# A decoder layer on one core: the two up-projections computed as three rounded products per block, delta net's first, with the samples' attention fold between two of their units

## The chip, the core and the metric

The kernel runs on one core of a Trainium2 chip. The core has five engines with instruction streams of their own: TensorE (PE, matrix products into the accumulator PSUM), VectorE (DVE), ScalarE (ACT), GpSimd (POOL) and SyncE (SP, which here only issues DMAs). They wait for each other by semaphores. The metric is the device time of one execution in microseconds (us): 2939.98 us, the median of 3 runs (2938.37 to 2940.77).

## What is computed

One layer of a hybrid decoder for 256 prompt tokens and 8 sample tokens, which go through all dense products together as T = 264 columns. Cut to what matters here:

```python
proj = rmsnorm(x) @ w_in                      # q, k, v, gates of both branches
o_fox = fox attention of the prompt, and of the samples against a paged cache
o_gdn = gated delta net, rmsnorm per head, times silu(z)
ga = sigmoid(proj[..., OFF_GATE:OFF_GATE + D_MODEL])
gb = sigmoid(proj[..., OFF_GATE + D_MODEL:N_IN])
m = ga * (o_fox @ w_up_fox) + gb * (o_gdn @ w_up_gdn)   # the two up-projections
x = x + m @ w_out
x = x + peer_ffn(rmsnorm(x))                  # routing, 16384 experts: "u" and "v"
x = x + sigmoid(rmsnorm(x) @ w_ple_gate) * (p @ w_ple)
```

`w_up_fox` and `w_up_gdn` are 1024 x 2048 each, `w_out` is 2048 x 2048.

## The kernel before

All activations lie transposed: 128 features on the partitions, the 264 tokens along a row. A dense product is worked off in units of 1 MB of weights (128 partitions x 2048 values). SP loads the units one after the other into a ring of four slots `WR`, in the order of the table `STREAM`: "A" (56 units), "gates" (32), "up" (16), "out" (16), "wq" (16), "u" (128), "v" (128), "ple" (16).

Nearly all of the stream is **split**. A unit is cut into four quarters of 512 columns. ACT writes each quarter rounded to fp32r into the buffer `ckh` (`high_part`, L431), DVE writes the rest, weight minus rounded weight, into `ckl` (`low_part`, L436), and PE makes three products for each block of 128 x 128: high by high, high by low, low by high (`products`, L626 to L628), on an input that is split in the same manner (`hh3`, `hl3`, in the tile `split`). There is one set of `ckh` and `ckl`: `high_part` of a quarter waits until PE has done with this quarter of the unit before (`quarter_done`), `low_part` waits for `hi_ready`, and PE waits for `lo_ready`. So a unit's high and low parts are made while PE works on the unit before it, a quarter behind.

The 16 units of "up" alone are not split. PE multiplies the unsplit float32 weights of the ring slot by the unsplit branch outputs `ot3` (L1050): of each unit 8 blocks are fox's and 8 delta net's, into two PSUM banks. Each unit makes one tile of 128 output features. DVE then multiplies both banks by their gates (L1895, L1896), adds them (L1899), ACT rounds the sum (L1307) and DVE makes its low part (L1901): the split input of "out". Only after the last tile does PE start "out" (`mt_ready`).

Just before "up", the attention of the samples is finished. PE multiplies the last pair of value pages (`value_pair(31)`, L946), DVE picks the rows (`value_rows(7)`, L1848 and L1851), PE folds them (job `sot`, L1038, 8 products with 8 columns each, which the trace shows as 16), DVE adds the sample's own value (L1879) and gives `of_ready`, for which PE, POOL (which then loads x again, L1429) and DVE wait.

What runs is fixed by the order in which each engine's program is written; a table of jobs gives the PSUM bank of each (`bank(n)` is bank n mod 4), and a job waits until the bank's last user, four jobs before, has been read (`claim`, `evac`). `rounded` is a second fp32r tile; while the gates run, its memory (under the name `early`) holds the recurrent states of the samples.

Of the kernel before, what the change touches and what calls it, by code (L numbers as in the profile page):

```python
# [49 lines left out]
for _name, _c in STREAM:  # L50
# [6 lines left out]
        22: [("gns", 1)], 23: [("gn0", 4)], 24: [("gn1", 4)], 31: [("sot", 1)]}  # L57
# [11 lines left out]
JOB_LIST += [("up", 16), ("out", 16),  # L69
            ("norm1", 1), ("wq", 16), ("key", 9), ("u", 128), ("norm2", 1), ("ple", 16)]  # L70
JOB = {}
SPLIT_JOBS = ("A", "out", "wq", "u", "ple") + tuple(f"gate{_u}" for _u in range(32))
# [10 lines left out]
def split_index(s):  # L83

    return s if s < S0["up"] else s - 16
# [69 lines left out]
def build(nc, xT, pT, wd, vd, wsmall, wple, subk, kx, vx, lx, state, convst, params, consts, ptab,  # L155
          o_x, o_k, o_v, o_lf, o_sp, o_ss, o_cs):
    with ExitStack() as ctx:
# [46 lines left out]
        as_f32 = lambda ap: ap.bitcast(F32)  # L204
        hh3 = sp_(HH, KT * T).rearrange("p (k t) -> p k t", t=T)
# [125 lines left out]
        merged, mh_ready = sem("merged"), sem("mh_ready")  # L331
        ws_hi, ws_lo = sem("ws_hi"), sem("ws_lo")
# [84 lines left out]
        def wait_slot(eng, it, m, s, back=0):  # L417

            if S0["up"] <= s < S0["out"]:
                eng.wait_ge(pe_job, it * m + (PJ[JOB["up"] + s - S0["up"]] - back))  # L420
            else:
                eng.wait_ge(lo_ready, it * (4 * m) + 4 * (split_index(s) + 1 - back))
# [186 lines left out]
        def _(pe):  # L609
# [20 lines left out]
            def split_unit(it, m, s, n, mj=4, h0=None):  # L630
# [4 lines left out]
                for q in range(RING):  # L635
                    wait_low_part(pe, it, m, s, q)
                    for kk in range(QK):
                        k = q * QK + kk
                        if h0 is not None:
                            pe.wait_ge(ht_ready, h0 + k + 1)  # L640
                        last = products(bank(n)[:, 0:T], ckh(q)[:, kk * P:(kk + 1) * P], ckl(q)[:, kk * P:(kk + 1) * P],
                                        hh3[:, k, :], hl3[:, k, :], k == 0, k == KT - 1)
                    last.then_inc(quarter_done, 1)

            def dense(name, its, h0=None):
                with pe.Fori(0, its) as it:
                    for j in range(RING):
                        split_unit(it, 4, S0[name] + j, JOB[name] + j, h0=None if j else h0)
# [385 lines left out]
            n = JOB["sot"]  # L1034
            claim(pe, n)
            pe.wait_ge(on_ready, NS)
            for s in range(NS):
                last = mm(bank(n)[:, s * NH:(s + 1) * NH], at(ON + s * P, P), cst(C_FOLD, NH), start=True, stop=True)  # L1038
            last.then_inc(pe_job, 1)


            pe.wait_ge(of_ready, 1)
            with pe.Fori(0, 4) as it:
                for j in range(RING):
                    n = JOB["up"] + j
                    pe.wait_ge(w_loaded[j], it * 16 + 16 * (S0["up"] // 4 + 1))
                    pe.wait_ge(evac[n % 4], it + n // 4)
                    for half in range(2):
                        for k in range(NH):
                            last = mm(ps[:, n % 4 + 4 * half, 0:T], wr(j)[:, (half * NH + k) * P:(half * NH + k + 1) * P],  # L1050
                                      ot3[:, half * NH + k, :], start=(k == 0), stop=(k == NH - 1))
                    last.then_inc(pe_job, 1)
            pe.wait_ge(mt_ready, 1)
            dense("out", 4)
# [63 lines left out]
        def _(act):  # L1118
# [161 lines left out]
            for u in range(32):  # L1280
# [13 lines left out]
                if u == 21:  # L1294
                    act.wait_ge(og_ready, 1)
                    wait_done(act, JOB["sgo13"] + 1)
                    for h in range(NH):
                        A(at(GSQ + h * T, T), blk(OT, NH + h), ACT.Square).then_inc(bsq_ready, 1)
                if u == 22:
# [4 lines left out]
            with act.Fori(0, 4) as it:  # L1304
                for j in range(RING):
                    act.wait_ge(merged, it * 4 + (j + 1))
                    A(split[:, bass.ds(it * (4 * T) + (HH + j * T), T)], at(TMU + (j % 2) * 2 * T, T), ACT.Copy).then_inc(mh_ready, 1)  # L1307
# [158 lines left out]
        def _(dve):  # L1466
# [387 lines left out]
            for u in range(32):  # L1854
# [20 lines left out]
            wait_evac(dve, JOB["spb"])  # L1875
            ch(V.tensor_tensor(at(OTMP, 64), at(VS, 64), at(PSF, 64), ALU.mult))
            n = JOB["sot"]
            wait_done(dve, n)
            V.tensor_tensor(ot3[:, 0:8, SEQ:T], hs(OTMP), bank(n)[:, 0:64].rearrange("p (s h) -> p h s", h=NH),  # L1879
                            ALU.add).then_inc(of_ready, 1)  # L1880
            dve.wait_ge(of_ready, 1)
            dve.sem_inc(evac[n % 4], 1)
            wait_evac(dve, JOB["gate31"])


            dve.wait_ge(of_ready, 1)
            V.memset(at(ZT, T), 0.0).then_inc(zero_tile, 1)
            with dve.Fori(0, 4) as it:
                for j in range(RING):
                    n = JOB["up"] + j  # L1890
                    dve.wait_ge(pe_job, it * 4 + PJ[n])
                    ga = arena[:, bass.ds(it * (4 * T) + (GT + j * T), T)]
                    gb = arena[:, bass.ds(it * (4 * T) + (GT + (16 + j) * T), T)]
                    m, t = at(TMU + (j % 2) * 2 * T, T), at(TMU + ((j % 2) * 2 + 1) * T, T)
                    V.tensor_tensor(t, gb, ps[:, 4 + n % 4, 0:T], ALU.mult).then_inc(mg_step, 1)  # L1895
                    V.tensor_tensor(m, ga, ps[:, n % 4, 0:T], ALU.mult).then_inc(evac[n % 4], 1)  # L1896
                    dve.wait_ge(mg_step, it * 8 + (2 * j + 1))
# [281 lines left out]
```

## Time and profile before

| | us |
|---|---|
| median of 3 runs | 2939.98 (2938.37 to 2940.77) |
| the profiled execution, its own time | 2936.59 |
| span of its trace, first to last instruction | 2934.9 |
| PE busy in the span | 2809.5 (96%) |
| DVE busy | 1784.8 (61%) |
| ACT busy | 1229.0 (42%) |
| POOL busy | 593.5 (20%) |

All times below are us from the start of the span. Busy shares are means over stages that differ, so the stages are read one by one: the gates end at about 926, "up" runs from 937 to 1054, "out" from 1058 to about 1152. In the rows, L with a number is the line of the kernel before; `ps` is PSUM, `arena` the large float32 tile, and an idle time in square brackets stands with the instruction that ended it and its releaser. The float32 product of L1050 is shown as two records for each block (512 for 256 blocks); a split block is three records, one for each of L626, L627 and L628. The granted clock of PE is 1.00 at 2.4 GHz and 0.50 at 1.2 GHz.

### The profile page before, as it was taken

The numbers are of one execution on the slowest core, as the hardware profiler recorded it, in microseconds if no ns is written. First come the engines' busy times: TensorE is split into PE (matmuls) and PEld (weight loads), VectorE is DVE, ScalarE is ACT, GpSimd is POOL, SyncE is SP. The second block draws the span as 40 slices with busy tenths as digits, with TensorE's granted clock in tenths as the row PEclk, the third lists the DMA queues.
The fourth block names the chain that finished last, engine by engine and source line by source line (L and its number), as shares of the span: only waits on it lengthen the run. The fifth ranks groups of instructions, "written<-read, shape, count | busy, mean of one in ns | idle before, by whom it ended". The sixth has DMA issues, their size and how long they took to land.

```text
span 2934.9 us, 57573 instructions
## 1 busy us (share of the span) xinstructions
PE 2809.5 (96%) x22051; PEld 2681.2 (91%) x22051; DVE 1784.8 (61%) x3445; ACT 1229.0 (42%) x2123; POOL 593.5 (20%) x457
## 2 busy tenths in 40 slices
PE   6999989989999998999999999996999999999989
PEld 5999957878877887999999999996999999999989
DVE  4467545655353245458886444443788888888854
ACT  4455432023332024444545444443444444444454
POOL 2100012000000000000477677773011111111000
PEclk8999969989999999999999999998999999999999
DMA  5455415545765466755677777776565666666533
GB/s 195 177 185 182 175 64 187 200 163 205 285 251 225 144 215 203 260 187 205 199 211 208 199 206 206 198 208 219 202 231 216 229 223 223 229 233 229 206 119 121
DMA packets 167186, 588.78 MB, mean 201 GB/s; under 512 B 53474, under 2 KB 86514, under 8 KB 114098
## 3 DMA queue, kind: packets, MB, share of 16 engines
q1 hardware_dynamic: 103234, 539.96, 52.1%
q0 software_dynamic: 45808, 26.10, 5.0%
q10 hardware_dynamic: 18048, 21.50, 2.1%
q8 instruction: 52, 0.85, 0.1%
q14 instruction: 44, 0.36, 0.0%
HBM read 543.36 MB, written 44.13 MB: 200 GB/s over the span
## 4 chain that ended last, share of the span: by engine, by line
PE 74%; POOL 14%; DMA 5%; issue 4%; DVE 3%; ACT 0%; SPq 0%; DVEq 0%; POOLq 0%; ACTq 0%
PE ps L626 20%; PE ps L627 19%; PE ps L628 19%; POOL gates L1439 14%; PE ps L1050 4%; DMA gates<-arena 4%; PE ps L860 2%; PE ps L946 1%; PE ps L702 1%; PE ps L686 1%; PE ps L621 1%; PE ps L847 1%; DVE arena L1479 1%; PE ps L983 1%; PE ps L678 1%
## 5 line engine op out<-in xcount | busy, mean ns | idle before, releaser
L436 DVE TENSOR_TENSOR split<-arena,split 128x512 fp32r<-128x512 f32 x1568 | 1140.2, 730 | 790.4 <-ACT split L431 780.0
L431 ACT ACTIVATE split<-arena 128x512 fp32r<-128x512 f32 x1568 | 987.3, 631 | 1259.7 <-PE ps L628 1259.3
L626 PE MATMUL ps<-split 128*128 128x264 f32 x4224 | 1216.9, 288 | 47.1 <-DVE split L436 41.6
L627 PE MATMUL ps<-split 128*128 128x264 f32 x4224 | 1207.0, 286 | 0.0
L628 PE MATMUL ps<-split 128*128 128x264 f32 x4224 | 1205.9, 285 | 0.0
L626 PEld LDWEIGHTS ps<-split 128*128 128x128 f32 x4224 | 806.0, 191 | 72.8 <-DVE split L436 35.6
L627 PEld LDWEIGHTS ps<-split 128*128 128x128 f32 x4224 | 806.7, 191 | 0.5
L628 PEld LDWEIGHTS ps<-split 128*128 128x128 f32 x4224 | 802.4, 190 | 0.0
L626 PE MATMUL ps<-rounded,split 128*128 128x264 f32 x2048 | 583.4, 285 | 26.5 <-DVE rounded L2057 26.5
L627 PE MATMUL ps<-rounded,split 128*128 128x264 f32 x2048 | 583.7, 285 | 0.0
L628 PE MATMUL ps<-rounded,split 128*128 128x264 f32 x2048 | 580.0, 283 | 0.0
L1439 POOL DMA_INDIRECT gates<-arena x264 | 436.1, 1652 | 421.4 <-DVE arena L2032 246.1
L626 PEld LDWEIGHTS ps<-rounded,split 128*128 128x128 f32 x2048 | 386.3, 189 | 26.7 <-issue 26.7
L627 PEld LDWEIGHTS ps<-rounded,split 128*128 128x128 f32 x2048 | 386.2, 189 | 0.0
L628 PEld LDWEIGHTS ps<-rounded,split 128*128 128x128 f32 x2048 | 385.7, 188 | 0.0
L2069 DVE TENSOR_TENSOR arena<-arena,ps 128x264 f32<-128x264 f32 x512 | 216.8, 423 | 0.0
L1462 POOL TENSOR_TENSOR arena<-arena 128x1056 f32<-128x1056 f32 x32 | 78.8, 2464 | 646.7 <-DMA arena<-gates 646.7
L1050 PE MATMUL ps<-arena 128*128 128x264 f32 x512 | 117.0, 391 | 0.7 <-DVE arena L1879 0.7
L1050 PEld LDWEIGHTS ps<-arena 128*128 128x128 f32 x512 | 98.4, 193 | 18.9 <-issue 0.8
L462 POOL DMA_DIRECT2D arena<-in_vx x32 | 16.9, 528 | 273.6 <-PE ps L946 240.3
L1387 POOL MEMSET early<- 128x3088 f32 x1 | 2.7, 2671 | 274.9 <-PE ps L628 274.9
L1307 ACT ACTIVATE split<-arena 128x264 f32 x16 | 6.8, 423 | 122.8 <-DVE arena L1899 122.8
(314 smaller groups left out, 1591.0 us busy)
## 6 DMA issues: line engine op xcount, KB each, us to landing
arena<-in_wd SPq DMA_DIRECT2D x280, 1024.0 KB, 5.6
arena<-in_vd SPq DMA_DIRECT2D x128, 1024.0 KB, 4.8
arena<-in_kx SPq DMA_DIRECT2D x64, 512.0 KB, 4.6
gates<-arena ACTq DMA_DIRECT2D x32, 528.0 KB, 3.2
acts<-arena SPq DMA_DIRECT2D x32, 528.0 KB
arena<-acts SPq DMA_DIRECT2D x32, 528.0 KB, 5.8
arena<-gates SPq DMA_DIRECT2D x32, 528.0 KB, 6.8
arena<-in_vx SPq DMA_DIRECT2D x32, 512.0 KB, 6.7
```

Source lines behind the costliest of these rows:

```text
L431: nc.scalar.activation(ckh(q), at(WR + (s % 4) * D_MODEL + q * QW, QW), ACT.Copy).then_inc(hi_ready, 1)
L436: nc.vector.tensor_tensor(ckl(q), at(WR + (s % 4) * D_MODEL + q * QW, QW), as_f32(ckh(q)), ALU.subtract).then_inc(lo_ready, 1)
L621: last = mm(bank(n)[:, 0:T], ones, blk(SQ, k), start=(k == 0), stop=(k == KT - 1))
L626: mm(out, wh, xh, start=start, stop=False)
L627: mm(out, wh, xl, start=False, stop=False)
L628: return mm(out, wl, xh, start=False, stop=stop)
L678: last = mm(bank(n)[0:count, 0:T], cst(C_SEL + 15 - b, count), at(base + (b % 4) * T, T), start=(b == 0), stop=(b == count - 1))
L860: last = mm(bank(n)[:, i * P:(i + 1) * P], at(lhs + o, P), at(rhs + o, P), start=True, stop=True)
L1050: last = mm(ps[:, n % 4 + 4 * half, 0:T], wr(j)[:, (half * NH + k) * P:(half * NH + k + 1) * P], ot3[:, half * NH + k, :], start=(k == 0), ...
L1439: pool.indirect_dma_start(gate_rows, bass.IndirectOffsetOnAxis(at(places, 1).bitcast(U32), 0), at(values, 1), None, compute_op=ALU.add).th ...
L1462: nc.gpsimd.tensor_tensor(a, a, at(WBUF + b * GRP, GRP), ALU.mult).then_inc(prod_ready, 1)
L2069: V.tensor_tensor(xt3[:, d, :], xt3[:, d, :], ps[:, 4 + q, 0:T], ALU.add).then_inc(y_added, 1)
```

## The change

"up" becomes part of the split stream, and `split_index` counts its units like all others. The host lays its weights out anew: 8 units of delta net's weights, then 8 of fox's. A unit now has 16 blocks of one branch, 8 for each of two tiles of output features, so it makes two jobs (`upg0` to `upg7`, `upf0` to `upf7`, two each).

The inputs have to be split for this. Delta net's: ACT copies 128 x 2112 values into `rounded` after gate 27 (the states that lay there must have been saved by then), DVE subtracts after gate 29's low parts. Fox's: ACT copies 128 x 2112 into `split`, DVE subtracts there (`attention_out`). This input is complete only when the samples' attention is; the fold `sot` now stands on PE behind unit 1 of delta net's half (`own_rows`).

In delta net's half DVE multiplies each tile by its gate in place. In fox's half it multiplies, adds delta net's part, and ACT and DVE split the sum as before. The split sum lies in two tiles now (`merged_high`, `merged_low`: blocks 0 to 7 in `split`, 8 to 15 in `rounded`).

```diff
-            pe.wait_ge(of_ready, 1)
-            with pe.Fori(0, 4) as it:
-                for j in range(RING):
-                    n = JOB["up"] + j
...
-                            last = mm(ps[:, n % 4 + 4 * half, 0:T], wr(j)[:, (half * NH + k) * P:(half * NH + k + 1) * P],
-                                      ot3[:, half * NH + k, :], start=(k == 0), stop=(k == NH - 1))
...
+            def up_unit(name, s, xh, xl):
+                for q in range(RING):
+                    n = JOB[name] + q // 2
+                    if q % 2 == 0:
+                        claim(pe, n)
+                    wait_low_part(pe, 0, 0, s, q)
+                    for kk in range(QK):
+                        k = (q % 2) * QK + kk
+                        last = products(bank(n)[:, 0:T], ckh(q)[:, kk * P:(kk + 1) * P], ckl(q)[:, kk * P:(kk + 1) * P],
+                                        xh(k), xl(k), k == 0, k == NH - 1)
+                    last.then_inc(quarter_done, 1)
+
+            pe.wait_ge(ol_split, 1)
+            for u in range(8):
+                up_unit(f"upg{u}", S0["up"] + u, lambda k: rd_(AH + k * T, T), lambda k: rd_(AL + k * T, T))
+                if u == 1:
+                    own_rows()
+            pe.wait_ge(ol_split, 2)
+            for u in range(8):
+                up_unit(f"upf{u}", S0["up"] + 8 + u, lambda k: hh3[:, k, :], lambda k: hl3[:, k, :])
...
+            for q in range(RING):
+                high_part(act, 0, 0, S0["up"], q)
+            for u in range(16):
+                for q in range(RING if u < 15 else 0):
+                    high_part(act, 0, 0, S0["up"] + u + 1, q)
+                if u == 2:
+                    act.wait_ge(of_ready, 1)
+                    A(sp_(HH, NH * T), at(OT, NH * T), ACT.Copy).then_inc(oh_split, 1)
+                for b in range(2 * (u - 8), 2 * (u - 8) + 2) if u >= 8 else ():
+                    act.wait_ge(merged, b + 1)
+                    A(merged_high(b), at(TMU + b % 2 * 2 * T, T), ACT.Copy).then_inc(mh_ready, 1)
...
+            def attention_out():
...
+                V.tensor_tensor(ot3[:, 0:8, SEQ:T], hs(OTMP), bank(n)[:, 0:64].rearrange("p (s h) -> p h s", h=NH),
+                                ALU.add).then_inc(of_ready, 1)
...
+                dve.wait_ge(oh_split, 2)
+                V.tensor_tensor(sp_(HL, NH * T), at(OT, NH * T), as_f32(sp_(HH, NH * T)), ALU.subtract).then_inc(ol_split, 1)
+                V.memset(at(ZT, T), 0.0).then_inc(zero_tile, 1)
+
+            for u in range(8):
+                for q in range(RING):
+                    low_part(dve, 0, 0, S0["up"] + u + 1, q)
+                for i in range(2):
+                    n, b = JOB[f"upg{u}"] + i, 2 * u + i
+                    wait_quarter(dve, 0, 0, S0["up"] + u, 2 * i + 1)
+                    V.tensor_tensor(blk(GT, 16 + b), blk(GT, 16 + b), bank(n)[:, 0:T], ALU.mult).then_inc(evac[n % 4], 1)
+                if u == 1:
+                    attention_out()
+            for u in range(8):
+                for q in range(RING if u < 7 else 0):
+                    low_part(dve, 0, 0, S0["up"] + 9 + u, q)
+                for i in range(2):
...
+                    V.tensor_tensor(t, blk(GT, b), bank(n)[:, 0:T], ALU.mult).then_inc(evac[n % 4], 1)
+                    wait_evac(dve, n)
+                    V.tensor_tensor(m, t, blk(GT, 16 + b), ALU.add).then_inc(merged, 1)
+                for b in range(2 * u, 2 * u + 2):
+                    dve.wait_ge(merged, b + 1)
+                    dve.wait_ge(mh_ready, b + 1)
+                    V.tensor_tensor(merged_low(b), at(TMU + b % 2 * 2 * T, T), as_f32(merged_high(b)), ALU.subtract).then_inc(mg_step, 1)
```

How this moves instructions is seen on three engines. First ACT, from the last gate on, before the change: L1286 is the gate's sigmoid, L1307 the rounding of a merged tile.

```order
L431 ACTIVATE split<-arena 128x512 [waits quarter_done,w_loaded3]
L431 ACTIVATE split<-arena 128x512 [waits quarter_done] x3
L1286 ACTIVATE arena<-ps 128x264 [waits quarter_done] x2
L1304 UNCONDITIONAL_BRANCH
L1304 ISA
L1307 ISA [waits merged]
```

ACT with the change, from the last gate (now L1301) on: L437 is `high_part`, four of it for a unit, L1333 the copy of fox's input.

```order
L1301 ACTIVATE arena<-ps 128x264 [waits quarter_done] x2
L437 ACTIVATE split<-arena 128x512 [waits quarter_done,w_loaded0]
L437 ACTIVATE split<-arena 128x512 [waits quarter_done] x3
L437 ACTIVATE split<-arena 128x512 [waits quarter_done,w_loaded1]
...
L437 ACTIVATE split<-arena 128x512 [waits quarter_done,w_loaded2]
...
L437 ACTIVATE split<-arena 128x512 [waits quarter_done,w_loaded3]
L437 ACTIVATE split<-arena 128x512 [waits quarter_done] x3
L1333 ACTIVATE split<-arena 128x2112 [waits of_ready]
```

ACT had nothing to split in "up"; now it does units 0 to 3 there (slots 0 to 3), and the copy for fox stands behind all four quarters of unit 3.

Next DVE at the same place, before the change: the last rows' choice, the own value, the fold's end, then the first merge.

```order
L1851 TENSOR_REDUCE arena<-arena 128x128 [waits dve_chain]
L1876 TENSOR_TENSOR arena<-arena 128x64 [waits evac2]
L1879 TENSOR_TENSOR arena<-arena,ps 128x8x8 [waits pe_job,dve_chain]
L1887 MEMSET arena 128x264 [waits of_ready,evac0]
L1888 UNCONDITIONAL_BRANCH
L1888 ISA
L1895 ISA [waits pe_job]
L1895 TENSOR_TENSOR arena<-arena,ps 128x264
```

DVE with the change, from the low parts of unit 2 (L442) to the gate products of unit 2 (L1930):

```order
L442 TENSOR_TENSOR split<-arena,split 128x512 [waits hi_ready] x4
L1930 TENSOR_TENSOR arena<-arena,ps 128x264 [waits quarter_done] x2
L1913 TENSOR_TENSOR arena<-arena 128x64 [waits evac2]
L1916 TENSOR_TENSOR arena<-arena,ps 128x8x8 [waits pe_job,dve_chain]
L1921 TENSOR_TENSOR split<-arena,split 128x2112 [waits of_ready,branch_high]
L1922 MEMSET arena 128x264
L442 TENSOR_TENSOR split<-arena,split 128x512 [waits hi_ready] x4
L1930 TENSOR_TENSOR arena<-arena,ps 128x264 [waits quarter_done] x2
```

The fold's end stands between the low parts of unit 2 and those of unit 3, and with it the subtraction for fox (L1921), which waits for ACT's copy.

Last PE before the change, at the end of the gates: L946 is the last value pair, L1038 the fold, L1050 the up-projection.

```order
L946 MATMUL ps<-arena 4x512 [waits vg_loaded7,vg_loaded6]
L946 MATMUL ps<-arena 4x512 x3
L1038 MATMUL ps<-arena 128x8 [waits on_ready,evac1]
L1038 MATMUL ps<-arena 128x8 x7
L1043 UNCONDITIONAL_BRANCH [waits of_ready]
```

PE with the change: L952 is the last value pair, L632 to L634 are the three products.

```order
L952 MATMUL ps<-arena 4x512 [waits vg_loaded7,vg_loaded6]
L952 MATMUL ps<-arena 4x512 x3
L632 MATMUL ps<-rounded,split 128x264 [waits lo_ready,evac1,branch_low]
L633 MATMUL ps<-rounded,split 128x264
L634 MATMUL ps<-rounded,split 128x264
```

The fold no longer stands between the last value pair and the first up-projection, nor does the wait for `of_ready`.

## Rows read from the trace of the kernel before

**Rows 1.** The page's chain of work that ended last, shares by engine and line
```profile
PE 74%; POOL 14%; DMA 5%; issue 4%; DVE 3%; ACT 0%; SPq 0%; DVEq 0%; POOLq 0%; ACTq 0%
PE ps L626 20%; PE ps L627 19%; PE ps L628 19%; POOL gates L1439 14%; PE ps L1050 4%; DMA gates<-arena 4%; PE ps L860 2%; PE ps L946 1%; PE ps L702 1%; PE ps L686 1%; PE ps L621 1%; PE ps L847 1%; DVE arena L1479 1%; PE ps L983 1%; PE ps L678 1%
```

**Rows 2.** PE's waits, longest: line and releaser, us, times, longest
```profile
PE ps L626 <- DVE rounded L2057: 26.5, 1, 26.5
```

**Rows 3.** Timeline, DVE's reads after "up" and "out": start, us, instruction
```profile
1047.21 0.43 DVE L1895 TENSOR_TENSOR arena<-arena,ps 128x264 f32<-128x264 f32 x1 [4.67 <-PE ps L1050]
...
1054.36 0.43 DVE L1895 TENSOR_TENSOR arena<-arena,ps 128x264 f32<-128x264 f32 x1 [4.75 <-PE ps L1050]
...
1072.53 0.42 DVE L1911 TENSOR_TENSOR arena<-arena,ps 128x264 f32 x1
...
1078.33 0.43 DVE L1911 TENSOR_TENSOR arena<-arena,ps 128x264 f32 x1
```

**Rows 4.** Groups of PE instructions by shape: count, busy us, mean ns
```profile
L1050 PE MATMUL ps<-arena 128*128 128x264 f32 x512 | 117.0, 391 | 0.7 <-DVE arena L1879 0.7
```

**Rows 5.** Timeline between the gates and "up", PE alone
```profile
929.97 1.05 PE L946 MATMUL ps<-arena 128*4 128x512 f32 x8 [2.81 <-DMA arena<-in_vx]
...
932.97 3.56 PE L1038 MATMUL ps<-arena 128*128 128x8 f32 x16 [1.95 <-DVE arena L1851]
...
937.20 3.44 PE L1050 MATMUL ps<-arena 128*128 128x264 f32 x7 [0.67 <-DVE arena L1879]
```

**Rows 6.** Timeline between "up" and "out", all engines
```profile
1054.71 0.42 DVE L1896 TENSOR_TENSOR arena<-arena,ps 128x264 f32<-128x264 f32 x1
1055.23 0.43 DVE L1899 TENSOR_TENSOR arena<-arena 128x264 f32<-128x264 f32 x1
1055.80 0.42 ACT L1307 ACTIVATE split<-arena 128x264 f32 x1 [6.80 <-DVE arena L1899]
...
1056.40 0.43 DVE L1901 TENSOR_TENSOR split<-arena,split 128x264 f32 x1 [0.73 <-ACT split L1307]
...
1057.80 0.47 PE L626 MATMUL ps<-split 128*128 128x264 f32 x1 [3.59 <-DVE split L436]
```

**Rows 7.** The chain, pieces in order of time near the gates: start, us, what
```profile
906.23 0.32 PE ps L626
...
912.22 0.97 PE ps L946 x8
```

**Rows 8.** Timeline, hand-over of one quarter from PE over ACT to DVE
```profile
918.92 0.28 PE L628 MATMUL ps<-split 128*128 128x264 f32 x1
...
919.24 0.63 ACT L431 ACTIVATE split<-arena 128x512 fp32r<-128x512 f32 x1 [0.83 <-PE ps L628]
...
919.90 0.69 DVE L436 TENSOR_TENSOR split<-arena,split 128x512 fp32r<-128x512 f32 x1 [0.76 <-ACT split L431]
```

**Rows 9.** Groups by shape: the widest copies on ACT and subtractions on DVE
```profile
L1202 ACT ACTIVATE arena<-arena 128x2112 f32<-128x2112 f32 x1 | 1.9, 1943 | 0.0
...
L2057 DVE TENSOR_TENSOR rounded<-arena,rounded 128x1056 fp32r<-128x1056 f32 x32 | 42.0, 1313 | 21.8 <-ACT rounded L1355 21.8
```

**Rows 10.** Stretches: busy PE, PEld, DVE, ACT, POOL; PEclk; DMA share, GB/s
```profile
932.00:933.00 1.00, 0.03 (x1) 0.06 (x1) 0.96 (x2) 0.00 (x0) 0.00 (x0) 0.50 1.05 434
...
940.00:942.00 2.00, 2.00 (x6) 1.59 (x5) 0.00 (x0) 0.00 (x0) 0.00 (x0) 0.52 0.89 372
942.00:944.00 2.00, 2.00 (x10) 1.70 (x10) 0.00 (x0) 0.00 (x0) 0.00 (x0) 1.00 0.99 422
```

**Rows 11.** The chain, pieces in order of time, single products of "out" after PE's wait
```profile
1058.27 0.22 PE ps L627
...
1061.54 0.12 PE ps L627
```

**Rows 12.** DMA issues of "up"'s first four weight units, and their landing
```profile
921.05 2.79 SPq L486 DMA_DIRECT2D arena<-in_wd  x4
...
DMA to landing us min/median/max: 6.5/9.4/12.3
```

More of the change, by code:

```diff
@@ L68 @@
     JOB_LIST += [(f"gate{_u}", 1)] + SLOT.get(_u, [])
-JOB_LIST += [("up", 16), ("out", 16),
+for _u in range(8):
+    JOB_LIST += [(f"upg{_u}", 2)] + ([("sot", 1)] if _u == 1 else [])
+for _u in range(8):
+    JOB_LIST += [(f"upf{_u}", 2)]
+JOB_LIST += [("out", 16),
             ("norm1", 1), ("wq", 16), ("key", 9), ("u", 128), ("norm2", 1), ("ple", 16)]
 JOB = {}
-SPLIT_JOBS = ("A", "out", "wq", "u", "ple") + tuple(f"gate{_u}" for _u in range(32))
+SPLIT_JOBS = ("A", *(f"up{_b}{_u}" for _b in "gf" for _u in range(8)), "out", "wq", "u", "ple") + tuple(f"gate{_u}" for _u in range(32))
 PJ = []
@@ L83, in split_index @@
 def split_index(s):
-    return s if s < S0["up"] else s - 16
+    return s
 def stream_of(n):
@@ L417, in wait_slot @@
         def wait_slot(eng, it, m, s, back=0):
[L419 to L422, printed above, removed]
+            eng.wait_ge(lo_ready, it * (4 * m) + 4 * (split_index(s) + 1 - back))
         def high_part(act, it, m, s, q):
@@ L1032, in _, with own_rows @@
                     output_norm(u - 22)
[L1034 to L1039, printed above, removed]
[L1042 to L1052 removed]
+            def own_rows():
+                n = JOB["sot"]
+                claim(pe, n)
+                pe.wait_ge(on_ready, NS)
+                for s in range(NS):
+                    last = mm(bank(n)[:, s * NH:(s + 1) * NH], at(ON + s * P, P), cst(C_FOLD, NH), start=True, stop=True)
+                last.then_inc(pe_job, 1)
@@ L1298, in _ @@
                         A(at(GSQ + h * T, T), blk(OT, NH + h), ACT.Square).then_inc(bsq_ready, 1)
+                if u == 27:
+                    for j in range(4):
+                        act.wait_ge(state_saved[j], 32)
+                    for b in range(4):
+                        wait_evac(act, JOB["gn1"] + b)
+                    A(rd_(AH, NH * T), at(OT + NH * T, NH * T), ACT.Copy).then_inc(oh_split, 1)
                 if u == 22:
@@ L1883, in _ @@
-            wait_evac(dve, JOB["gate31"])
[L1886 to L1897, printed above, removed]
-                    dve.wait_ge(evac[n % 4], it + (n // 4 + 1))
-                    V.tensor_tensor(m, m, t, ALU.add).then_inc(merged, 1)
-                    dve.wait_ge(mh_ready, it * 4 + (j + 1))
-                    V.tensor_tensor(split[:, bass.ds(it * (4 * T) + (HL + j * T), T)], m,
-                                    as_f32(split[:, bass.ds(it * (4 * T) + (HH + j * T), T)]), ALU.subtract).then_inc(mg_step, 1)
@@ L1904, in _ @@
+            dve.wait_ge(mg_step, 16)
             dve.sem_inc(mt_ready, 1)
```

48 lines of the change are left out of this document (27 added, 21 removed).

## The prediction

> **What bounds the kernel now.** I began with the chain of work that ended last [rows 1]: three quarters of it is PE, nearly all in the split products L626 to L628. The float32 up-projection L1050 is 4%, the only dense stage that is not split. So here PE's own time is the price, and DVE and ACT, at 61% and 42% busy, matter only where PE waits for them.
>
> The chain has one stretch that is not PE's: POOL's scatter L1439 (14%), all through "u", after which PE waits 26.5 us before "v" [rows 1, 2]. Does a gain in "up" survive that? The scatter is fed by routing, which DVE does between the low parts of "u"; all this starts from the end of "out". Nothing in it is tied to an earlier clock, so it moves with the stage, and I count a gain or a loss in "up" in full.
>
> Then I read the stage itself in the timeline. One float32 unit takes 1054.36 - 1047.21 = 7.15 us, one split unit of "out" 1078.33 - 1072.53 = 5.80 us, between reads of the same kind [rows 3]. Both hold 16 blocks: 512 records of L1050 are 256 blocks, 16 units of 16 [rows 4]. The split unit is the shorter one although it is three products.
>
> Last come the seams. Before "up", PE ends the last value pair at 929.97 + 1.05 = 931.02, waits for DVE, does the fold from 932.97 on, waits again and starts "up" at 937.20 [rows 5]. Behind "up" it waits 3.59 us and starts "out" at 1057.80 [rows 6]. From the end of the last value pair to "out" are thus 1057.80 - 931.02 = 126.8 us. This is the stretch that I work out anew.
>
> **The change part by part.**
>
> *The products.* 16 units at 5.80 us are 92.8 us (16 at 7.15 were 114.4). Here DVE and ACT must keep up. In delta net's half DVE has four low parts at 0.69 and two gate products at about 0.43 [rows 8, 3], 3.6 us of 5.80. Fox's half is tighter, so I follow one hand-over from the end of a unit: ACT's last quarter starts 0.04 later and takes 0.63, to 0.67; DVE's low part takes 0.69 and starts 0.03 later, to 1.39 [rows 8]. Then gate product (0.43, to 1.82), sum (0.10 hand-over and 0.43, to 2.35), second gate product (0.35 more, to 2.70), sum (to 3.23), ACT's rounding (0.14 and 0.42, to 3.79) [rows 6]. Only now does ACT start the first quarter of the unit after next (to 4.42), and DVE follows after its own merged low part (0.18 after ACT's rounding, 0.43: to 4.40), done at about 5.1. PE wants it at 5.80. So PE sets the pace with 0.7 us to spare, and I cost these additions at nothing. If this cover is gone, each further us costs up to 8 us, one for each fox unit.
>
> The Trainium skill, "FP8 and Floating Point Precision", section TensorE Precision Notes, counts a true float32 product as four passes. Three products instead of four passes would take 114.4 us to 85.8 us rather than 92.8. The rows say otherwise: 7.15 to 5.80 is a ratio of 0.81, not 0.75, and the 5.80 is measured on the same three products. I stay with the rows.
>
> *The seam in front.* The fold and both waits for DVE go from between value pair and "up". Unit 0's high and low parts need the weights: issued from 921.05 on, landing after 6.5 us at best and 12.3 at worst, median 9.4 [rows 12]. If the first issued lands first, at 927.6, ACT and DVE have its first quarter ready at about 929 and the last at about 931, so PE can go on at 931.02. Switching from float32 back to split products shows one product of 0.32 instead of 0.12 [rows 7, 11]: 0.2 us. If the first load were the slow one (12.3: 933.4), PE would wait until about 934.8, some 4 us more.
>
> *The fold, moved behind unit 1.* All its 16 records are paid on PE, without the DVE waits around them: `value_rows(7)` is long done by then, and unit 2's low parts are ready. At half clock they took 3.56 us [rows 5, 10]. At full clock the nearest row is eight small products in 0.97 [rows 7], so 16 take 1.9 us; with 0.2 for the switch back 2.1 us. The bounds are 2.1 and 3.8.
>
> *The split of delta net's input* (ACT 2112 columns after gate 27, DVE after gate 29). ACT's only copy of this width took 1.94 us, and DVE's 1056 columns about 1.3 us (mean) [rows 9]; for 2112 I estimate 2.4 us from the 0.69 for 512 and a little under twice 1.31. Both engines have over 2.5 us free in each gate unit of about 7 us (912.22 - 906.23 is 6.0 for the products and 0.97 for the value pair [rows 7]). Hidden; the cost is 0.
>
> *The split of fox's input: a new wait.* In DVE's order, as the rows of the change show it, the subtraction L1921 stands behind unit 2's low parts and ahead of unit 3's. It waits for ACT's copy L1333. In ACT's order this copy stands behind the four quarters of unit 3, and the fourth of those may only be written when PE has done with unit 2's fourth. So while PE does unit 2, DVE stands still, and when PE ends unit 2, no low part of unit 3 exists. From there on, one behind the other: hand-over 0.04, ACT's fourth quarter 0.63, the copy 1.94, hand-over 0.18, DVE's subtraction 2.4, the memset (264 columns; at most the 0.43 of other operations of that width [rows 6], taken as 0.2), the low part of unit 3's first quarter 0.69, and a hand-over to PE as short as that from it, 0.04 [rows 8, 9, 6]. Sum 6.1 us in which PE has nothing to do. Nothing else covers it: PE's next work in order is unit 3. Its other three quarters then come at 0.69 or less each, faster than PE's 5.80 / 4 = 1.45.
>
> *PE's clock.* In the seam before "up" the granted clock stood at 0.50 from 932 on and came back to 1.00 only at 942 [rows 10]. After the wait before "out", products come 0.22 apart instead of 0.12, from 1058.3 to 1061.5 [rows 11]: some 16 products that cost 0.1 us more each, 1.6 us. I expect one such dip after the 6.1 us wait, and one at the start of "up" (PE has been idle before the last value pair as it was: 2.81 us [rows 5]). Two dips are 3.2 us. A third after the fold is possible. Bounds: 0 and 4.8.
>
> *The seam behind.* One gate product less stands after PE's last product: it took 1054.71 - 1054.36 = 0.35 us [rows 3, 6]. 3.59 - 0.35 = 3.2 us. What POOL loads at `of_ready` (x again) starts later than before by roughly 10 us, and is wanted by DVE only in "out", some 90 us on: hidden.
>
> *Sum* from the end of the last value pair to "out": 0.2 + 92.8 + 2.1 + 6.1 + 3.2 + 3.2 = 107.6 us, against 126.8. That is 19.2 us less. The profiled execution took 2936.59 us, which makes 2917.4; the median of the runs is 3.39 us above the profiled one, so for a median I forecast **2920.8 us**.
>
> **The rivals.**
>
> *No wait at unit 3, or a smaller one* (and no dips): 0.2 + 92.8 + 2.1 + 3.2 = 98.3, 28.5 us less, 2911.5. The order of the rows of ACT and DVE speaks against it; for it would speak only that I misread which quarter the copy waits for. The rule of the four passes, which for the products would give 85.8, belongs here too: 7.0 less than my sum, 2913.8. Together 8%.
>
> *Fox's half falls to the pace of DVE and ACT.* The loop from unit end to the first low part crosses some ten hand-overs; with 0.15 more in each it is 6.6 and the unit grows by 0.8 to 1.5 us, 6 to 12 us in all: 2927 to 2933. For it: the spare is only 0.7 us. Against: all pieces are taken from rows. 14%.
>
> *Unit 0's weights come late*: 4 us more, 2925. 6%.
>
> *The saving does not appear*: what the split unit saves (1.35 us a unit, 21.6 in all) is eaten, because in the new, unrolled place products come no faster than 0.149 us apart, the pace of 7.15 us a unit. Then the stage is 19.2 - 21.6 = 2.4 us slower, 2942, no change by the measure below. The gates are unrolled too, and run a unit in 6.0 us [rows 7]. 4%.
>
> *Slower than before: the clock stays low.* If after the wait at unit 3 the clock did not come back within some 3 us, each us at 0.50 would cost 0.5 us. To eat 19.2 us and be 5.9 us slower takes 50 us at half clock, which is five units' work done at twice 5.80, so it decides from about the fourth slow unit behind unit 3; with all 13 that follow it is 13 x 5.8 = 75 us, less the 1.6 that the sum has for this dip: 2994. For it: before "up" the clock was low for about 10 us. Against: that was with the sparse fold in it; under split products it came back in 3.2 us [rows 11]. 2%.
>
> **How the numbers follow.** A measurement of this kernel can tell some 0.2% (5.9 us) from no change. Chances: the forecast 66%, no wait or faster products 8%, fox's half at DVE's pace 14%, late weights 6%, no saving 4%, clock 2%. The range takes in the dips (3.2 less, 1.6 more), the fold (1.7 more), late weights (4 more) and most of the loop's price upwards; 2914 to 2930. Faster, that is below 2934.1: all cases but the last two, 94%, of which I move two to "same" for what lies above the top of the loop's price. Faster 0.92, same 0.06, slower 0.02.
>
> **What would show it.** The reads of DVE in the new stage 5.80 us apart, for a pair of tiles, in both halves: right on the products and the loop; 6.5 or more in fox's half: the second rival. One idle time of PE of about 6 us, ended by DVE's low part, behind unit 2: right on the new wait; none, or one under 3 us, and I misread the order. "up" starting at about 931 and the fold taking some 2 us after 943: right on the front seam. Product spacing of 0.22 for some 3 us after the wait: the dip. If "out" starts outside 1033 to 1048, the prediction is wrong.

## The result and the profile after

The changed kernel takes 2914.39 us, the median of 6 runs (2910.62 to 2917.08); the kernel before took 2937.65 us beside it (6 runs, 2928.01 to 2940.77). The ratio is 0.9928, with a 95% interval of 0.9917 to 0.9939: faster by 0.7%, where 0.65% was forecast (2920.8 us), and only 0.4 us above the lower end of the range (2914 to 2930). The profiled execution took 2914.9 us, its span is 2913.2 us, so 21.7 us less than before.

First the page. The chain that ended last, shares of the span by engine and by line, answers to [rows 1]:

```profile
PE 73%; POOL 14%; DMA 5%; issue 4%; DVE 3%; ACT 1%; SPq 0%; POOLq 0%; DVEq 0%; ACTq 0%
PE ps L632 21%; PE ps L633 20%; PE ps L634 20%; POOL gates L1468 14%; DMA gates<-arena 4%; PE ps L866 2%; PE ps L952 1%; PE ps L708 1%; PE ps L692 1%; PE ps L853 1%; PE ps L627 1%; DVE arena L1508 1%; PE ps L989 1%; PE ps L684 1%; DVE split L1512 1%
```

The 4% of the float32 line are gone, and the three split products (now L632 to L634) have grown from 58% to 61%. ACT is rounded to 1% where it was rounded to 0%: two steps of ACT in the new wait, 2.5 us together in the chain below, lift it over the rounding. Of PE's waits in the whole span (us in total, times, longest) one line answers to [rows 2]:

```profile
PE ps L632 <- DVE rounded L2101: 26.6, 1, 26.6
```

It was 26.5. POOL's 14% in "u" did move along with the stage, and the gain reaches the end: from the start of "out" to the end of the span there are 2913.2 - 1037.69 = 1875.5 us, before 1877.1.

The pace, that is DVE's reads of the tiles in delta net's half (L1930) and in fox's (L1940), from the timeline (start, us, instruction), answers to [rows 3]:

```profile
966.51 0.76 DVE L1930 TENSOR_TENSOR arena<-arena,ps 128x264 f32<-128x264 f32 x2
972.31 0.76 DVE L1930 TENSOR_TENSOR arena<-arena,ps 128x264 f32<-128x264 f32 x2
...
995.51 0.42 DVE L1940 TENSOR_TENSOR arena<-arena,ps 128x264 f32<-128x264 f32 x1
...
1001.31 0.42 DVE L1940 TENSOR_TENSOR arena<-arena,ps 128x264 f32<-128x264 f32 x1
```

A unit takes 5.80 us in both halves, to the hundredth. Now the seam in front and the fold, in the chain of the stretch (start, us, what), which answers to [rows 5]:

```profile
929.73 1.39 PE ps L952 x8
931.12 0.52 PE ps L632
...
933.62 0.22 PE ps L633
933.84 0.13 PE ps L634
...
944.12 1.69 PE ps L1045 x16
945.81 0.22 PE ps L632
```

The last value pair ends at 931.12, and unit 0 starts at once. Its first 11 products are spaced as at half clock: 0.52, then ten times 0.22. The fold, at full clock between units 1 and 2, takes 1.69 us where it took 3.56, and nothing waits around it. Behind unit 2, further down the same chain, stands the new wait:

```profile
951.75 0.63 ACT split L437
952.38 1.86 ACT split L1333
954.26 2.36 DVE split L1921
956.63 0.28 DVE arena L1922
956.91 0.55 DVE split L442
...
957.59 0.56 PE ps L632
958.15 0.22 PE ps L633
```

ACT's fourth quarter, the copy for fox, DVE's subtraction, the memset, the first low part: one behind the other, as the prediction's sum has them, and PE stands still for 5.9 us. The products after it are 0.22 apart until 961.0. In the stretches (us, busy PE, PEld, DVE, ACT, POOL, then the granted clock, DMA share and GB/s) the clock shows the same:

```profile
953.00:955.00 2.00, 0.00 (x0) 0.00 (x0) 0.74 (x1) 1.23 (x1) 0.00 (x0) 0.80 0.95 406
955.00:957.00 2.00, 0.00 (x0) 0.00 (x0) 1.99 (x3) 0.00 (x0) 0.00 (x0) 0.50 0.06 25
...
959.00:961.00 2.00, 2.00 (x11) 2.00 (x10) 0.93 (x3) 0.33 (x1) 0.00 (x0) 0.50 0.20 41
961.00:963.00 2.00, 2.00 (x19) 2.00 (x18) 0.70 (x2) 0.93 (x2) 0.00 (x0) 0.99 0.99 401
```

It falls within the idle time and is back at 961. Last the seam behind, from the timeline; it answers to [rows 6]:

```profile
1037.69 0.39 PE L632 MATMUL ps<-split 128*128 128x264 f32 x1 [2.90 <-DVE split L442]
```

2.90 us where there were 3.59, and the products of "out" that follow come 0.12 apart at once: the slow start that "out" had before [rows 11] does not occur here.

From the end of the last value pair to "out" are 1037.69 - 931.12 = 106.6 us; before 126.8, forecast 107.6.

### The profile page after: what moved, and what is told of

It is laid out like the page before. It is cut to its first block, busy times and chain, and to the rows that moved or that the text cites. A ratio compares the mean times of both kernels' runs of the same rounds, so it can differ in the third digit from the quotient of the medians.

```text
span 2913.2 us, 58039 instructions
## 1 busy us (share of the span) xinstructions
PE 2783.4 (96%) x22307; PEld 2675.7 (92%) x22307; DVE 1828.4 (63%) x3511; ACT 1270.9 (44%) x2189; POOL 593.7 (20%) x457
## 4 chain that ended last, share of the span: by engine, by line
PE 73%; POOL 14%; DMA 5%; issue 4%; DVE 3%; ACT 1%; SPq 0%; POOLq 0%; DVEq 0%; ACTq 0%
PE ps L632 21%; PE ps L633 20%; PE ps L634 20%; POOL gates L1468 14%; DMA gates<-arena 4%; PE ps L866 2%; PE ps L952 1%; PE ps L708 1%; PE ps L692 1%; PE ps L853 1%; PE ps L627 1%; DVE arena L1508 1%; PE ps L989 1%; PE ps L684 1%; DVE split L1512 1%
## 5 line engine op out<-in xcount | busy, mean ns | idle before, releaser
L442 DVE TENSOR_TENSOR split<-arena,split 128x512 fp32r<-128x512 f32 x1632 | 1180.9, 727 | 825.6 <-ACT split L437 816.6
L437 ACT ACTIVATE split<-arena 128x512 fp32r<-128x512 f32 x1632 | 1026.2, 631 | 1308.4 <-PE ps L634 1307.0
L632 PE MATMUL ps<-split 128*128 128x264 f32 x4224 | 1218.0, 288 | 46.4 <-DVE split L442 40.9
L634 PE MATMUL ps<-split 128*128 128x264 f32 x4224 | 1206.9, 286 | 0.0
L632 PEld LDWEIGHTS ps<-split 128*128 128x128 f32 x4224 | 807.1, 191 | 72.2 <-DVE split L442 34.7
L634 PEld LDWEIGHTS ps<-split 128*128 128x128 f32 x4224 | 803.5, 190 | 0.0
L632 PE MATMUL ps<-rounded,split 128*128 128x264 f32 x2304 | 657.7, 285 | 32.5 <-DVE rounded L2101 26.6
L633 PE MATMUL ps<-rounded,split 128*128 128x264 f32 x2304 | 657.4, 285 | 0.0
L634 PE MATMUL ps<-rounded,split 128*128 128x264 f32 x2304 | 653.6, 284 | 0.0
L632 PEld LDWEIGHTS ps<-rounded,split 128*128 128x128 f32 x2304 | 435.9, 189 | 34.1 <-issue 34.1
L633 PEld LDWEIGHTS ps<-rounded,split 128*128 128x128 f32 x2304 | 435.6, 189 | 0.0
L634 PEld LDWEIGHTS ps<-rounded,split 128*128 128x128 f32 x2304 | 434.9, 189 | 0.0
L2101 DVE TENSOR_TENSOR rounded<-arena,rounded 128x1056 fp32r<-128x1056 f32 x32 | 42.0, 1312 | 22.0 <-ACT rounded L1384 22.0
L866 PEld LDWEIGHTS ps<-arena 128*128 128x128 f32 x448 | 50.5, 191 | 3.0 <-issue 3.0
```

The costliest lines, as they stand in the source:

```text
L437: nc.scalar.activation(ckh(q), at(WR + (s % 4) * D_MODEL + q * QW, QW), ACT.Copy).then_inc(hi_ready, 1)
L442: nc.vector.tensor_tensor(ckl(q), at(WR + (s % 4) * D_MODEL + q * QW, QW), as_f32(ckh(q)), ALU.subtract).then_inc(lo_ready, 1)
L632: mm(out, wh, xh, start=start, stop=False)
L633: mm(out, wh, xl, start=False, stop=False)
L634: return mm(out, wl, xh, start=False, stop=stop)
L866: last = mm(bank(n)[:, i * P:(i + 1) * P], at(lhs + o, P), at(rhs + o, P), start=True, stop=True)
```

## The experiments

Runs of one kernel differ by some us before "up" is even reached: the last gate's sigmoid starts anywhere from 922.97 to 930.50 in the traces below. So beside the runs' medians I read the stage itself, from the start of that sigmoid to the first product of "out". Before it is 1057.80 - 926.22 = 131.6 us, with the change 1037.69 - 924.91 = 112.8. Each run has one trace, so a stage is a single reading; the changed kernel was traced twice, and its two stages differ by 0.6 us. The lines L in a run's rows are those of that run's kernel.

**The changed kernel once more**, beside the experiments on the subtraction, on the fold and on the value pair, on their chip. The other four ran on a second chip, without the changed kernel beside them.

> The changed kernel as it is, beside the others on one chip. Some 21 us under the kernel before, as in its first measurement (ratio 0.9928). PE's wait behind unit 2 of the up-projections should again be near 5.9 us and 'out' should start near 1037.7 of the span.

2915.04 us (4 runs), the kernel before there 2936.62; ratio 0.9923 (0.9900 to 0.9945). The stage takes 1041.67 - 929.47 = 112.2 us. PE's waits in the stage repeat themselves; of the 8.8 us, 5.9 stand behind unit 2 and 2.9 before "out":

```profile
PE ps L632 <- DVE split L442: 8.8, 2, 5.9
```

**DVE's subtraction later.** Only DVE's order is changed: the subtraction for fox stands behind unit 3's gate products, so that unit 3's low parts need not wait for it.

```diff
+                V.memset(at(ZT, T), 0.0).then_inc(zero_tile, 1)
+
+            def fox_low():
                 dve.wait_ge(oh_split, 2)
                 V.tensor_tensor(sp_(HL, NH * T), at(OT, NH * T), as_f32(sp_(HH, NH * T)), ALU.subtract).then_inc(ol_split, 1)
-                V.memset(at(ZT, T), 0.0).then_inc(zero_tile, 1)
...
                 if u == 1:
                     attention_out()
+                if u == 3:
+                    fox_low()
```

> One step of DVE is moved: the subtraction that makes the low part of fox's input goes from behind unit 1's gate products to behind unit 3's; the fold's end and the memset stay. Theory (the order of DVE's program makes the wait: low parts of unit 3 stand behind a subtraction that waits for ACT's copy): PE's 5.85 us wait behind unit 2 goes, and with it the clock's dip behind it (1.6 us); 7.4 us less than the changed kernel, no wait over 0.5 us between units 2 and 15. Rival (the wait is ACT's: its copy of 1.95 us keeps it from the high parts, or the weights of unit 3 are late): a wait of 2 us or more stays behind unit 2 or 3 and under 4 us are saved.

2909.35 us (4 runs), ratio 0.9904 (0.9880 to 0.9927); this interval overlaps that of the changed kernel, so the gain over it is read from the traces. PE's waits between 915 and 1045:

```profile
PE ps L632 <- DVE split L442: 2.9, 1, 2.9
PE ps L952 <- DMA arena<-in_vx: 2.7, 1, 2.7
```

The wait behind unit 2 is gone entirely, not merely halved, and with it its slow start. The stage takes 1029.75 - 926.00 = 103.8 us, 8.4 less than the changed kernel on this chip: the wait of 5.9, its dip, which is 2.1 in that trace (18 products at half clock), and 0.4 in front of the fold. A change of DVE's order alone removes the wait, and nothing hid under it. That ACT's order has to be as it is, too, is shown below, where the copy is moved instead.

**The fold back in front of unit 0.** On PE `own_rows` stands before unit 0 again, with DVE's part of it; the rest is as in the changed kernel.

```diff
+            own_rows()
             pe.wait_ge(ol_split, 1)
             for u in range(8):
                 up_unit(f"upg{u}", S0["up"] + u, lambda k: rd_(AH + k * T, T), lambda k: rd_(AL + k * T, T))
-                if u == 1:
-                    own_rows()
```

> One part of the change is undone: the fold of the samples' attention stands again between the last value pair and the first up-projection, and DVE adds the own value there; all else as changed, the subtraction for fox too. Theory (the fold's new place saves the wait for DVE's choice of rows and lets it run at full clock): PE waits about 1.9 us for the rows, the fold takes about 3.0 instead of 1.7, unit 0 starts at about 936 instead of 931.1, and the wait behind unit 2 stays near 5.9, so 3.2 us slower than the changed kernel (2.5 to 4.5). Rival (the place of the fold is worth nothing, since DVE would have been late anyway): within 1 us of it.

2921.54 us (4 runs), ratio 0.9945 (0.9928 to 0.9961). The chain at the seam:

```profile
935.30 0.70 DVE arena L1876
936.03 1.03 DVE arena L1879
...
937.20 3.56 PE ps L1045 x16
```

L1876 and L1879 are here the choice of the rows. PE waits 2.0 us for the rows again, and the fold takes the 3.56 us of before [rows 5], because the clock is low there. The wait behind unit 2 stays (5.7). The stage is 1046.53 - 930.50 = 116.0 us, 3.8 more than in the changed kernel beside it, 3.2 more than in its first trace. So moving the fold alone is worth 3 to 4 us, as expected (2.5 to 4.5), half of it by the clock at which it runs: 3.56 to 1.69. The fold was expected at 3.0.

**Float32 products in the new order.** The units, the fold and both splits of the inputs stay where the change has put them; only PE multiplies the unsplit weights by the unsplit inputs, with the high and low parts made but not used, and SP frees a slot when PE has done with it.

```diff
-                        last = products(bank(n)[:, 0:T], ckh(q)[:, kk * P:(kk + 1) * P], ckl(q)[:, kk * P:(kk + 1) * P],
-                                        xh(k), xl(k), k == 0, k == NH - 1)
+                        last = mm(bank(n)[:, 0:T], wr(s % 4)[:, (q * QK + kk) * P:(q * QK + kk + 1) * P], ot3[:, x0 + k, :],
+                                  start=(k == 0), stop=(k == NH - 1))
```

> Undoes the split products alone: PE again multiplies unsplit float32 weights by the unsplit branch outputs, in the new order, the new units and with the fold between units 1 and 2; ACT and DVE still make all high and low parts, which are not used in 'up', and SP loads a slot again only when PE is through with the unit. Theory (the products are worth 1.35 us a unit, the rest of the gain is the seams'): units 7.1 to 7.2 us apart, 'up' 20 to 22 us longer than in the changed kernel, PE's wait behind unit 2 unchanged at about 5.9: about level with the kernel before, within 3 us. Rival (the gain came mainly from the new order and the seam): units under 6.5 us or the total 10 us or more under the kernel before.

2937.41 us (10 runs) against 2936.53; ratio 1.0003 (0.9986 to 1.0021): no gain is left that these runs could tell, that is, none over some 4 us. The chain:

```profile
931.52 16.65 PE ps L1057 x64
948.17 1.68 PE ps L1046 x16
949.85 7.27 PE ps L1057 x32
```

A unit takes 7.27 us here (the first two, begun at half clock, 8.3 each), a little over the 7.1 to 7.2 expected and the 7.15 of before; why, the runs don't show. The fold and the wait behind unit 2 have the same sizes as with split products. From the end of the last value pair to "out" are 1060.87 - 931.52 = 129.4 us, 22.8 more than with the split products and 2.6 more than before. So the net gain of the change is the products' pace; what the fold and the seams bring, the new wait and its dip take back. This is the prediction's own balance: the products save 21.6 us, and the sum comes to 19.2.

**Two products instead of three.** In "up" the product of high weights by the input's low part is left out, so "up" is computed less exactly. PE then has two thirds of the work, and what DVE and ACT can do at most comes to light.

```diff
-                        last = products(bank(n)[:, 0:T], ckh(q)[:, kk * P:(kk + 1) * P], ckl(q)[:, kk * P:(kk + 1) * P],
-                                        xh(k), xl(k), k == 0, k == NH - 1)
+                        mm(bank(n)[:, 0:T], ckh(q)[:, kk * P:(kk + 1) * P], xh(k), start=(k == 0), stop=False)
+                        last = mm(bank(n)[:, 0:T], ckl(q)[:, kk * P:(kk + 1) * P], xh(k), start=False, stop=(k == NH - 1))
```

> Leaves out one of the three products of each up-projection block (high weight by low input); all else as in the changed kernel. It takes PE's cover away, so that the pace of ACT and DVE shows. Theory (PE sets the pace of both halves; in fox's half DVE, with 5.1 us of work for a unit and its hand-overs, comes next): delta net's units 3.9 us apart (32 products at 0.121), fox's 5.2 to 5.6, so PE now waits for low parts in each fox unit; some 18 us less than the changed kernel. Rival (DVE and ACT have ample time in fox's half too): 3.9 to 4.2 in both halves, 28 us or more less. Second rival (they were at the limit): fox's units stay at 5.8.

2896.6 us in its one run, 17.8 less than the changed kernel's first median. DVE's reads, first in delta net's half, then in fox's:

```profile
962.80 0.76 DVE L1930 TENSOR_TENSOR arena<-arena,ps 128x264 f32<-128x264 f32 x2
966.71 0.76 DVE L1930 TENSOR_TENSOR arena<-arena,ps 128x264 f32<-128x264 f32 x2
...
978.45 0.42 DVE L1940 TENSOR_TENSOR arena<-arena,ps 128x264 f32<-128x264 f32 x1
...
983.58 0.42 DVE L1940 TENSOR_TENSOR arena<-arena,ps 128x264 f32<-128x264 f32 x1
```

Delta net's half follows PE: 3.91 us a unit, two thirds of 5.80 (3.87). Fox's does not: 5.13. One turn of it in the chain shows who sets this pace:

```profile
978.53 0.35 DVE arena L1940
...
979.72 0.45 DVE arena L1942
...
980.19 0.43 ACT split L1336
...
980.72 0.43 DVE split L1946
...
981.17 2.50 DVE split L442 x4
983.66 0.35 DVE arena L1940
```

Gate products and sums (the last one shown), ACT's rounding, the merged low part, four low parts, and the next unit's gate product: DVE's own turn, without PE. It takes 5.13 us, just under the 5.2 to 5.6 expected, and neither 3.9 to 4.2 nor 5.8. So the rival that fox's half falls to the pace of DVE and ACT was real, and missed by 0.67 us; and a faster PE would win only 0.67 us a unit there.

That this is so near the 0.7 of the prediction is in part luck, for the prediction added up another loop: from the end of a unit on PE over ACT's last quarter, the gate products and ACT's rounding to the first low part of the unit after next, 5.1 us. The changed kernel's own timeline shows this one:

```profile
1004.02 1.90 DVE L442 TENSOR_TENSOR split<-arena,split 128x512 fp32r<-128x512 f32 x3
...
1005.83 0.63 ACT L437 ACTIVATE split<-arena 128x512 fp32r<-128x512 f32 x1 [0.80 <-PE ps L634]
```

The first of the three low parts is done by 1004.71 (0.69 each), and PE ends the unit before it just ahead of 1005.83: some 4.7 us after the last unit's end, with 1.1 to spare.

**ACT's copy earlier.** A second way to shorten the wait: on ACT the copy for fox stands ahead of unit 3's high parts, DVE's order is unchanged.

```diff
-                for q in range(RING if u < 15 else 0):
-                    high_part(act, 0, 0, S0["up"] + u + 1, q)
                 if u == 2:
                     act.wait_ge(of_ready, 1)
                     A(sp_(HH, NH * T), at(OT, NH * T), ACT.Copy).then_inc(oh_split, 1)
+                for q in range(RING if u < 15 else 0):
+                    high_part(act, 0, 0, S0["up"] + u + 1, q)
```

> One step of ACT is moved: the copy of fox's input goes from behind unit 3's four high parts to ahead of them; DVE's order stays as in the changed kernel. Theory (the wait behind unit 2 is the chain of ACT's fourth quarter, copy, subtraction, low part, which only starts when PE ends unit 2): copy and subtraction now run while PE does unit 2, DVE is free some 5.3 us after unit 2's start, and PE's wait falls from 5.85 to under 1 us. Rival (DVE's subtraction in front of the low parts is too long by itself): 2.5 us or more stay.

2913.5 us in its one run, whose gates ended late (930.46). PE's waits in its stage are 3.1 us, 2.9 of them before "out":

```profile
PE ps L632 <- DVE split L442: 3.1, 2, 2.9
```

So 0.2 us are left behind unit 2, and no dip follows: the stage takes 1035.25 - 930.46 = 104.8 us. The copy and the subtraction now run while PE does unit 2 (951.38 to 955.74 in its chain); without ACT's fourth quarter in front of them nothing of them is late. So either order alone can be changed, and both ways out leave the wait at 0.2 us or nothing: it took the copy behind ACT's fourth quarter and the subtraction ahead of DVE's low parts together, as the prediction had it. Of the rivals named for it none is left.

**The last value pair behind unit 0.** With the subtraction moved later as above (here behind unit 4), PE does unit 0 before the last value pair, whose page it waits for (2.7 us); the fold goes one unit further back, and so does the copy on ACT.

```diff
-                if u == 31:
-                    value_pair(31)
...
-                if u == 1:
+                if u == 0:
+                    value_pair(31)
+                if u == 2:
                     own_rows()
```

> As with the subtraction moved later, and besides the last value pair of the samples' attention stands on PE behind unit 0 of the up-projections, its rows' choice behind it on DVE, the fold behind unit 2, the copy for fox one unit later on ACT and the subtraction behind unit 4. Theory (PE's idle time before the up-projections is the wait for the last value page, which shares the DMA engines with four weight units): PE goes on as soon as unit 0's first quarter is split, at about 927.7, the pair costs 1.2 us behind unit 0, unit 0 and pair are done at about 934.7 instead of 938.3; 3.5 us less than with the subtraction alone, 11 us less than the changed kernel. Rival (weights and page come together, the wait only changes its name): less than 1 us gained over the subtraction alone.

2909.32 us (4 runs), ratio 0.9908 (0.9891 to 0.9924), the stage 1026.56 - 922.97 = 103.6: nothing against the 103.8 with the pair in front, where 3.5 less was expected; the rival was right. The chain says where it went:

```profile
917.81 6.78 DMA arena<-in_wd
924.61 0.64 ACT split L437
925.27 0.70 DVE split L442
...
926.11 0.36 PE ps L632
...
933.70 0.97 PE ps L952 x8
```

PE no longer waits for the page, but for unit 0's weights, their split included, until 926.1; the clock falls in unit 0 all the same (it takes 933.70 - 926.11 = 7.6 us instead of 5.8), and the pair is paid later, 0.97 and some 0.2 for the switch behind it. One transfer's wait was traded for another's.

**The page before the weights.** Page and weights are loaded at the same time, so here SP holds back the weights of units 1 to 3 until the last page has landed; the subtraction stands later as above.

```diff
-            loop(S0["up"], 88, 4)
+            for j in range(RING):
+                if j == 1:
+                    sp.wait_ge(vg_loaded[PAGES - 1], 16 * NS)
+                wait_slot(sp, 0, 0, S0["up"] + j - RING)
+                load_w(0, 0, S0["up"] + j, wd, 88 + j)
...
```

> As with the subtraction moved behind unit 3, and besides SP holds back the weights of units 1 to 3 until the last value page has landed. Theory (PE's 2.7 to 3.9 us wait for this page is its sharing of the DMA engines with 4 MB of weights; unit 1's weights have some 5 us to spare): the page and unit 0 land at about the time the gates end, PE's wait for the page falls under 1 us, unit 0 starts 3.5 us earlier after the last gate and there is no dip of the clock at its start; 3 to 5 us less than with the subtraction alone. Rival (the page is slow by itself, or units 1 to 3 now come late): under 1 us gained, or a new wait behind unit 0.

2905.3 us (4 runs, 2901.05 to 2906.1), ratio 0.9901 (0.9868 to 0.9934). The chain in front, with the page's transfer first (before, and with the subtraction later alone, 8.37 and 8.25 us):

```profile
921.43 6.99 DMA arena<-in_vx
...
928.55 1.05 PE ps L960 x8
929.60 0.32 PE ps L640
...
941.40 1.69 PE ps L1053 x16
```

The page takes 6.99 us, PE waits 1.4 instead of 2.7 (under 1 was expected), and the clock does not fall: pair 1.05 instead of 1.89, unit 0 without slow products. The stage takes 1027.28 - 926.18 = 101.1 us, 2.7 less than with the subtraction alone on the other chip, just short of the 3 to 5 expected. The page needs most of its time even so: holding back 3 MB of weights saved 1.3 us of it. Among the versions with all products this stage is the shortest: 11.7 us less than the change, 30.5 less than before. By its runs alone it can be told from the kernel before, but its interval overlaps those of the subtraction alone and of the changed kernel.

## Why the prediction was right, point by point

- **What bounds the stage**: right. PE's pace sets it, and the float32 run shows that without the split products no net gain is left.
- **The products**, 16 units at 5.80 us: right to the hundredth. The rule of four passes for a true float32 product (the Trainium skill, "FP8 and Floating Point Precision", section TensorE Precision Notes) would by an estimate have made three quarters of the old pace of it, 85.8 us for the 16 units; the trace shows 92.8. The ratio 0.81 belongs to this kernel's float32 pace of 7.15 us.
- **The new wait**, forecast 6.1, measured 5.9 us, link by link the one that was added up; taken away in two ways, it went but for 0.2 us.
- **The dips**, forecast two with 3.2 us and 0.2 for the switch: measured in the spacing of the products 0.4 + 10 x 0.1 = 1.4 at unit 0, the switch in it, and some 1.8 behind the wait, 3.2 together. The first was smaller than forecast, the second larger.
- **The fold**, forecast 2.1, measured 1.69 and 0.1 for the switch. The bound of 3.8 was for half clock; it ran at full. The price came from products of another shape (4 x 512, where the fold has 128 x 8), so that it was near is luck.
- **The seam behind**, forecast 3.2, measured 2.9 us: besides the gate product that stands there no longer, the steps from the last one to PE are 0.2 shorter.
- **The loop of fox's half**: held. Its spare was sized a little low, at 0.7 us; the changed kernel's timeline has 1.1, and DVE's own turn, with 0.67, is the nearer limit.
- **The split of delta net's input**: hidden, as forecast. The two wide operations take 1.96 and 2.35 us, the value pairs around them still come 6.97 us apart, and PE waits for nothing between 880 and 925. The second load of x lands at about 957 and is read from 1045 on.
- **Unit 0's weights**: in time; the first split starts at 926.33, the value pair ends at 931.12.

The sum with what was measured is 92.8 + 3.2 + 1.8 + 5.9 + 2.9 = 106.6, as read directly. The terms that were off were off by 0.4 us at most.

What the sum didn't have is "out": I counted its slow start as before. Of the span's 21.7 us, 20.2 come from the stretch that I summed, 1.6 from "out" starting at full clock, and 0.1 went in front. This last figure hides two that cancel by chance: in this trace the last gate ended 1.3 us earlier than before, but the last value page took 9.43 us instead of 8.37. Read from the last gate on, the stage gained 18.8 us, and 19.4 in the second trace. That the runs' median fell by 23.3 us instead is within what they scatter.

## What to carry to other kernels

Where the same product runs elsewhere in the kernel in another form, the distance of two reads behind it is the price of a unit, and it carries over; then the work is in the seams. Of each step that is squeezed between two units, write down what the other engines have queued behind it: here one subtraction at the wrong place in DVE's order cost 7.7 us (5.9 and the dip) of the 22.8 that the products gave, and moving it changes a few lines. A stage that is read from one landmark to another in the traces tells differences of 3 us that whole runs hide.

## What was not expected of the hardware

When PE has been idle for 2.9 us before "out", the clock sometimes falls and sometimes not, in the same place with the same wait. In both traces of the changed kernel, with the subtraction later and with the fold in front, "out" starts and runs on at full clock. In the run with the pair behind unit 0 PE idles 2.9 us as well, and this is what its stretches show:

```profile
1026.00:1029.00 3.00, 2.44 (x11) 2.44 (x12) 2.31 (x4) 1.14 (x3) 0.00 (x0) 0.50 0.00 0
1029.00:1032.00 3.00, 3.00 (x15) 3.00 (x15) 0.69 (x1) 0.63 (x1) 0.00 (x0) 0.50 0.59 246
```

The clock is 0.50 for 6 us there. What this costs is seen at DVE's first read of a tile of "out", first in the changed kernel, then in that run:

```profile
1045.08 0.42 DVE L1955 TENSOR_TENSOR arena<-arena,ps 128x264 f32 x1
```

```profile
1036.73 0.42 DVE L1960 TENSOR_TENSOR arena<-arena,ps 128x264 f32 x1
```

The first comes 7.39 us after the start of "out" (1037.69), the second 10.17 (1026.56): 2.8 us more. "out" with all that follows takes 1879.9 us instead of 1875.5; the other 1.6 us come behind "out", and the clock at this seam does not explain them. With the page before the weights and with ACT's copy earlier the clock falls at this place too, in the float32 run about 1 us after "out" has begun; there the first read comes 8.7 to 8.9 us after the start. What decides it the runs don't show; it stays open, with a price of 1.3 to 2.8 us at this seam.
